# Output, up and down projections of a gated block: from plain tiled products to seven half-size block products in one sequence over all tokens

## The reference

```
h = RMSNorm(x)
q_a | k_a | v_a | u_pool | q_mem = h @ w_in
y_attn = window attention; y_pool = pooling; y_mem = attention into mem
merged = sum_i sigmoid(h @ Wg_i + b_i) * (y_i @ w_branch_i)
x = x + merged @ w_out                                  # 1024 x 1024
x = x + relu(RMSNorm(x) @ w_up)**2 @ w_down             # 1024 x 4096, 4096 x 1024
out = RMSNorm(x)
```

## Time and profile before

| | |
|---|---|
| median of 3 runs | 2945.35 us (2944.4 to 2946.05) |
| the profiled execution, its time | 2946.49 us |
| its span, first to last instruction | 2944.8 us |
| PE busy | 2890.6 us (98%) |
| DVE, ACT, POOL busy | 1350.5, 961.5, 195.3 us |
| DMA | 293.99 MB, mean 100 GB/s |
| mean granted TensorE clock | 0.995 |

### The profile page before, as it was taken

The page is one execution under the profiler, slowest core; times in us unless marked ns, Lnnn a source line. Parts: engine busy times, 40 slices in busy tenths (PEclk is TensorE's granted clock), DMA queues, the critical chain, the costliest instruction groups (busy, mean ns, idle before and its releaser), DMA issues.

```text
span 2944.8 us, 35670 instructions
## 1 busy us (share of the span) xinstructions
PE 2890.6 (98%) x13481; PEld 2391.0 (81%) x13481; DVE 1350.5 (46%) x1625; ACT 961.5 (33%) x1425; POOL 195.3 (7%) x191
## 2 busy tenths in 40 slices
PE   8999999999999999999999999999999999999998
PEld 7788888888778888888877888888887888888886
DVE  4643344445364245444446334544444632454444
ACT  5542332222353233212245323322224432422223
POOL 0101110000010111000001011000000001100000
PEclk9999999999999999999999999999999999999999
DMA  5123333332322342333232234223323222432332
GB/s 187 61 83 97 121 122 100 100 98 88 101 62 86 100 157 86 100 100 100 86 102 69 79 100 157 91 95 100 100 86 102 69 86 93 157 99 88 99 100 86
DMA packets 290347, 293.99 MB, mean 100 GB/s; under 512 B 9704, under 2 KB 285212, under 8 KB 290204
## 3 DMA queue, kind: packets, MB, share of 16 engines
q1 hardware_dynamic: 287900, 283.71, 30.3%
q0 software_dynamic: 2304, 8.39, 0.7%
HBM read 283.67 MB, written 8.39 MB: 99 GB/s over the span
## 4 chain that ended last, share of the span: by engine, by line
PE 90%; issue 5%; DVE 2%; POOL 1%; ACT 1%; DMA 0%; DVEq 0%; POOLq 0%; ACTq 0%
PE ps L993 29%; PE ps L995 28%; PE ps L994 28%; PE ps L998 1%; POOL sq_sum L971 1%; PE ps L1145 1%; PE ps L1128 1%; PE ps L1116 1%; PE ps L1089 0%; ACT sq L357 0%; DVE u_lo L806 0%; DVE scores L733 0%; DVE out_tm L897 0%; DVE scores L715 0%; DVE h_lo L656 0%
## 5 line engine op out<-in xcount | busy, mean ns | idle before, releaser
L993 PE MATMUL ps<-h_hi,w_hi 128*128 128x512 f32 x2240 | 885.2, 395 | 12.7 <-issue 12.7
L995 PE MATMUL ps<-h_hi,w_lo 128*128 128x512 f32 x2240 | 874.7, 390 | 0.0
L994 PE MATMUL ps<-h_lo,w_hi 128*128 128x512 f32 x2240 | 874.4, 390 | 0.0
L615 DVE TENSOR_TENSOR w_lo<-stage,w_hi 128x2048 fp32r<-128x2048 f32 (+1 forms) x269 | 559.6, 2080 | 641.6 <-ACT w_hi L357 641.6
L357 ACT ACTIVATE w_hi<-stage 128x2048 fp32r<-128x2048 f32 (+2 forms) x287 | 485.1, 1693 | 526.0 <-PE ps L995 524.6
L993 PE MATMUL ps<-u_hi,w_hi 128*128 128x512 f32 x1280 | 501.0, 391 | 5.5 <-DVE u_lo L806 5.5
L993 PEld LDWEIGHTS ps<-h_hi,w_hi 128*128 128x128 f32 x2240 | 422.3, 189 | 101.9 <-issue 14.3
L995 PE MATMUL ps<-u_hi,w_lo 128*128 128x512 f32 x1280 | 498.4, 389 | 0.0
L994 PE MATMUL ps<-u_lo,w_hi 128*128 128x512 f32 x1280 | 498.1, 389 | 0.0
L995 PEld LDWEIGHTS ps<-h_hi,w_lo 128*128 128x128 f32 x2240 | 422.1, 188 | 88.8
L994 PEld LDWEIGHTS ps<-h_lo,w_hi 128*128 128x128 f32 x2240 | 422.6, 189 | 86.7 <-issue 1.0
(11 more groups left out here) (153 smaller groups left out, 1837.9 us busy)
## 6 DMA issues: line engine op xcount, KB each, us to landing
stage<-in_w_up SPq DMA_DIRECT2D x128, 512.0 KB, 4.7
stage<-in_w_down SPq DMA_DIRECT2D x128, 512.0 KB, 4.0
stage<-in_w_gate SPq DMA_DIRECT2D x96, 512.0 KB, 4.5
stage<-in_w_in SPq DMA_DIRECT2D x60, 512.0 KB, 4.8
stage<-in_w_out SPq DMA_DIRECT2D x32, 512.0 KB, 4.1
x_tm<-in_x SPq DMA_DIRECT2D x5, 2048.0 KB, 9.6
stage<-in_w_branch_attn SPq DMA_DIRECT2D x32, 256.0 KB, 4.0
stage<-in_w_branch_pool SPq DMA_DIRECT2D x32, 256.0 KB, 3.0
```

The source lines that it names most:

```text
L615: v.tensor_tensor(w_lo[:, slot, 0:kt, :], stage[:, slot, 0:kt, :], w_hi[:, slot, 0:kt, :].bitcast(F32), ALU.subtract).then_inc(lo_done, 1)
L993: mm(dst, wh, xh, start=first, stop=False)
L994: mm(dst, wh, xl, start=False, stop=False)
L995: return mm(dst, wl, xh, start=False, stop=last)
```

## The change

The four blocks now stop after the merge (32 pieces in a block). POOL stores each block's merged tiles to DRAM (`mrg_d`). `x_next` brings the next block's rows during the merge, and their eight transposes follow the last merge piece. The factor 0.5 of the merge moves into the halves of the branches.

After the four blocks a second part does the three projections for all tokens, in straight-line code: seven jobs (`FIRST`), 72 pieces. Job 0 is `w_out` (8 pieces), jobs 1 and 2 are `w_up` for one half of the tokens each (16 pieces each), jobs 3 to 6 are quarters of `w_down`'s rows (8 pieces each). A job keeps a 1024 x 1024 operand resident; a piece is the other operand's 1024 x 256 columns, and gives 256 x 1024 of output. Both are cut into 2 x 2 blocks, and the output is made from seven block products instead of eight (the scheme of sums of Strassen in Winograd's form). A block product is four k-tiles of `product`, 12 matmuls with 512 columns. The seven are named after the piece's block or sum of blocks: A11, S2, S1, S3, A12, A22, S4, in this order on PE.

- POOL makes the piece's sums S1 to S4 (`s_sums`) and, for jobs 0 and 3 to 6, adds the four output tiles to the rows (`add_tile`), which are loaded from and stored to DRAM (`load_rows`, `store_rows`). ACT and DVE make the halves of the seven piece blocks (`s_split`, `s_low`; six slots). DVE takes the products out of PSUM (`take_u2`, `take_c22`, `take_c11`, `take_c21`, `take_c12`), and in jobs 1 and 2 also squares the positive part of four tiles (`relu_sq`), which SP stores to `up_d`.
- For a job, the resident operand comes in four quarters: three into `src`, the fourth, B21, into `res_raw`. DVE makes T1 and T2 (`t1`, `t2`), POOL T3 and T4 (`t3`, `t4`, 128x2048 elements each), and ACT and DVE make the halves of the seven resident blocks (`r_split`, `r_low`, 128x2048 each). Quarter 0 is issued when two pieces of the job before are left, quarters 1 and 2 in the last piece, B21 after its product A12.
- Pieces of `piece_f` have one buffer: the next is issued when all sums of the one before are made and its first six blocks are split. SP's queue is in order: in jobs 3 to 5 the store of the finished rows stands ahead of it and waits for POOL's four additions (`row_add`).
- Job 0's rows are normalised (`scale_tile`), transposed by PE (`rows_across`, 16 transposes a piece) and stored to `ht_d`; the last job's rows are normalised and stored to the output.

The core of the diff:

```diff
-W_MERGE, W_OUT, W_MLP = 16, 32, 36
-PIECES = 68
+W_MERGE = 16
+PIECES = 32
 PIECES0 = 4
 
...
+N_OUT, N_UP, N_DOWN = 8, 16, 8
+FIRST = [0, 8, 24, 40, 48, 56, 64]
+NQT = 72
+SLOTS = 6
+PROD = 7
+A11, S2, S1, S3, A12, A22, S4 = range(PROD)
...
+    res_hi = sb("res_hi", [P, PROD, 4, TB], F32R)
+    lo_at = off[0]
+    res_lo = sb("res_lo", [P, PROD, 4, TB], F32R)
+    res_raw = at("res_raw", [P, PROD, 4, TB], F32, lo_at)
+    src = sb("src", [P, 3, 4, TB])
+    piece_f = sb("piece_f", [P, KT, PC])
+    s_hi = sb("s_hi", [P, SLOTS, 4, P], F32R)
+    s_lo = sb("s_lo", [P, SLOTS, 4, P], F32R)
+    s_sum = sb("s_sum", [P, 2, 4, P])
...
+    S_SRC = {A11: quarter(0, 0), S2: s_sum[:, 1], S1: s_sum[:, 0], S3: quarter(0, 1), A12: quarter(1, 0), A22: quarter(1, 1),
+             S4: s_sum[:, 1]}
+    R_SRC = {0: src[:, 0], 1: src[:, 0], 2: res_raw[:, 2], 3: src[:, 1], 4: res_raw[:, 4], 5: res_raw[:, 5], 6: src[:, 2]}
+    S_NEED = {S1: 1, S2: 2, S3: 3, S4: 4}
+    R_HI_ORDER = (0, 2, 1, 3, 4, 6, 5)
+    R_LO_ORDER = (0, 1, 2, 3, 6, 4, 5)
+    U2, U3, U4, C22, C11, C21, C12 = range(1, 8)
+    FREED = {S2: U2, S1: C22, S3: U3, A12: C11, A22: C21, S4: C12}
+    def acc(n, i):
+        return ps[:, (PROD * n + i) % 6, :]
...
-                    load(j % 2, w_outv[:, :, j * PC:(j + 1) * PC], lo0 + (W_OUT + j))
-                    sp.wait_ge(tile_done, t0 + (G_MERGE if j < 2 else G_OUT + 4 * (j - 2) + 2))
-                    sp.wait_ge(x_ld, 16)
-                    sp.dma_start(xres[:, j % 2], x_rows[:, bass.ds(row_q, TT), j * PC:(j + 1) * PC])\
-                        .then_inc(xres_ld[j % 2], 16)
-                sp.wait_ge(tile_done, t0 + G_OUT)
-                sp.wait_ge(x_ld, 16)
-                sp.dma_start(x_tm[:], x_rows[:, bass.ds(row_n, TT), :]).then_inc(x_ld, 16)
...
+                        sp.wait_ge(tile_done, t0 + G_MERGE)
+                        sp.dma_start(x_next[:], x_rows[:, bass.ds(row_n, TT), :]).then_inc(x_ld, 16)
...
+            sp.wait_ge(phase, 3)
+            for j in range(4):
+                sp.wait_ge(mrg_st[j], 16 * NBLK)
+            sp.wait_ge(x_ld, 16 * (NBLK + 1))
...
+            load_quarter(0, 0)
+            load_piece(0)
+            load_quarter(0, 1)
+            load_quarter(0, 2)
+            load_b21(0)
+            load_rows(0)
+            for n in range(NQT + 1):
+                if squares(n - 1):
+                    store_up(n - 1, 3, c12, 0, 1)
+                if adds_rows(n - 1) and not is_final(n - 1):
+                    sp.wait_ge(row_add, 4 * row_quartets(n))
+                    store_rows(n - 1, rows_v)
+                if n + 1 < NQT:
+                    sp.wait_ge(s_lo_done, PROD * n + 6)
+                    sp.wait_ge(s_done, 4 * n + 4)
+                    load_piece(n + 1)
+                if is_final(n - 1):
+                    sp.wait_ge(fin_rdy, n - FIRST[6])
+                    store_rows(n - 1, out_v)
...
+                if adds_rows(n + 1) and not 0 < n < N_OUT:
+                    m = n + 1
+                    if m >= FIRST[3]:
...
+                    sp.wait_ge(row_st[row_slot(m)], 16 * slot_uses(m))
+                    load_rows(m)
+                if n < NQT and starts(n + 2):
+                    j = job_of(n) + 1
+                    sp.wait_ge(r_lo_done, PROD * j)
+                    sp.wait_ge(t_pool, 2 * j)
+                    if j < 3:
+                        for s in range(2):
+                            sp.wait_ge(ht_st[s], 16 * 4 * j)
+                    load_quarter(j, 0)
+                if n + 1 < NQT and starts(n + 1):
+                    load_quarter(job_of(n + 1), 1)
+                    load_quarter(job_of(n + 1), 2)
+                if squares(n):
+                    store_up(n, 0, c22, 1, 1)
+                    store_up(n, 1, c11, 0, 0)
+                if n + 1 < NQT and starts(n + 1):
+                    sp.wait_ge(prod, PROD * n + A12 + 1)
+                    load_b21(job_of(n + 1))
...
+            def s_split(n, i):
+                g = PROD * n + i
+                if n >= NQT:
+                    return
+                if i == 0:
+                    act.wait_ge(pc_ld, 16 * (n + 1))
+                if i in S_NEED:
+                    act.wait_ge(s_done, 4 * n + S_NEED[i])
+                if g >= SLOTS:
+                    act.wait_ge(prod, g - SLOTS + 1)
+                op(s_hi[:, ring_slot(n, i)], S_SRC[i], ACT.Copy).then_inc(s_hi_done, 1)
+            def r_split(j, s):
+                if s in (0, 6):
+                    act.wait_ge(src_ld[0 if s == 0 else 2], 16 * (j + 1))
+                elif s == 4:
+                    act.wait_ge(b21_ld, 16 * (j + 1))
+                elif s in (1, 2):
+                    act.wait_ge(t_done, 2 * j + (2 if s == 1 else 1))
+                else:
+                    act.wait_ge(t_pool, 2 * j + (1 if s == 3 else 2))
+                if j:
+                    act.wait_ge(prod, PROD * (FIRST[j] - 1) + s + 1)
+                op(res_hi[:, s], R_SRC[s], ACT.Copy).then_inc(r_hi_done, 1)
...
+            def s_low(n, i):
+                if n >= NQT:
+                    return
+                dve.wait_ge(s_hi_done, PROD * n + i + 1)
+                slot = ring_slot(n, i)
+                v.tensor_tensor(s_lo[:, slot], S_SRC[i], s_hi[:, slot].bitcast(F32), ALU.subtract).then_inc(s_lo_done, 1)
+            def r_low(j, s):
+                dve.wait_ge(r_hi_done, PROD * j + R_HI_ORDER.index(s) + 1)
+                if s == 4:
+                    dve.wait_ge(t_pool, 2 * j + 2)
+                elif s == 2:
+                    dve.wait_ge(t_done, 2 * j + 2)
+                v.tensor_tensor(res_lo[:, s], R_SRC[s], res_hi[:, s].bitcast(F32), ALU.subtract).then_inc(r_lo_done, 1)
+            def t1(j):
+                for i in range(2):
+                    dve.wait_ge(src_ld[i], 16 * (j + 1))
+                if j:
+                    dve.wait_ge(prod, PROD * (FIRST[j] - 1) + S1 + 1)
+                v.tensor_tensor(res_raw[:, 2], src[:, 1], src[:, 0], ALU.subtract).then_inc(t_done, 1)
+            def t2(j):
+                dve.wait_ge(src_ld[2], 16 * (j + 1))
+                dve.wait_ge(r_lo_done, PROD * j + 1)
+                dve.wait_ge(t_done, 2 * j + 1)
+                v.tensor_tensor(src[:, 0], src[:, 2], res_raw[:, 2], ALU.subtract).then_inc(t_done, 1)
...
+            def take_u2(n):
+                dve.wait_ge(prod, PROD * n + S2 + 1)
+                dve.wait_ge(ev_act, n + 1)
+                if adds_rows(n - 1):
+                    dve.wait_ge(row_add, 4 * row_quartets(n))
+                v.tensor_tensor(u2[:], p1[:], acc(n, S2), ALU.add).then_inc(ev_dve, 1)
+            def take_c22(n):
+                dve.wait_ge(prod, PROD * n + S3 + 1)
+                dve.wait_ge(ev_dve, 7 * n + U2)
+                v.tensor_tensor(u3[:], u2[:], acc(n, S3), ALU.add).then_inc(ev_dve, 1)
+                dve.wait_ge(ev_dve, 7 * n + U3)
+                v.tensor_tensor(u2[:], u2[:], acc(n, S1), ALU.add).then_inc(ev_dve, 1)
+                if squares(n - 1):
+                    dve.wait_ge(up_st[0], 16 * up_quartets(n))
+                v.tensor_tensor(c22[:], u3[:], acc(n, S1), ALU.add).then_inc(ev_dve, 1)
...
+            for n in range(NQT):
+                j, first, last = job_of(n), starts(n), starts(n + 1) and n + 1 < NQT
+                if first:
+                    r_low(j, 3)
+                s_low(n, 6)
+                take_u2(n)
+                if last:
+                    r_low(j + 1, 0)
+                    t1(j + 1)
...
+                if has_norm(n - 1):
+                    row_var(n - 1)
+                s_low(n + 1, 0)
+                if has_norm(n - 1):
+                    scale_tile(n - 1)
+                if first:
+                    r_low(j, 6)
+                    r_low(j, 4)
+                    r_low(j, 5)
+                take_c22(n)
+                if last:
+                    t2(j + 1)
+                relu_sq(n, C22)
+                s_low(n + 1, 1)
+                s_low(n + 1, 2)
+                take_c11(n)
+                relu_sq(n, C11)
+                if last:
+                    r_low(j + 1, 1)
+                take_ht(n - 1, 0)
+                s_low(n + 1, 3)
+                take_c21(n)
+                relu_sq(n, C21)
+                take_ht(n - 1, 1)
+                s_low(n + 1, 4)
+                if last:
+                    r_low(j + 1, 2)
+                take_c12(n)
+                relu_sq(n, C12)
+                s_low(n + 1, 5)
...
+                    pool.wait_ge(sum_rdy, sj + 5)
+                    pool.dma_start(mrg_v[:, 2 * j:2 * j + 2, bass.ds(b * TB, TB)], resid[:, 2 * j:2 * j + 2, :])\
+                        .then_inc(mrg_st[j], 16)
...
+                add_tile(n - 1, C12, 0, 1)
+                if first:
+                    t4(j)
+                row_rms(n - 1)
+                s_sums(n + 1, S1)
+                s_sums(n + 1, S2)
+                s_sums(n + 1, S3)
```

(41 more changed lines are left out.)

709 lines of the change are left out of this document (397 added, 312 removed).

## The result

The changed kernel takes 3029.19 us (median; 3023.81 to 3030.45) where the kernel before took 2945.7 on the same chip: ratio 1.028, 95% interval 1.0262 to 1.0298. The forecast was 2969 us, +0.8%. The time lies within the stated range (2865 to 3035), but the change costs 83 us where the sum had about 23. The sign and most of the walk hold; the stalls are 60 us more than the sum had.

What follows compares the result with a forecast made beforehand. Bound taken: TensorE's count of matmuls. First part 1314.4, start 59, 71 pieces 1351.1, stalls 24 + 26 + 10 + 156, clock 13, end 14 sum to 2967.5, plus 1.7 outside the span: 2969 us; range 2865 to 3035.

Steps and rivals of the forecast that it cites:

- the term of job 0: Job 0's pieces: 16 transposes cost 2.1 us a piece and waits about 1, so 8 x 3 = 24 us.
- the lower clock: TensorE's clock halves after idling: 2.2 us lost at each boundary that no later wait absorbs, 13 us in all.
- the rows' store before `scale_tile`: A wait not walked; the prediction called itself wrong if it held DVE in every piece; no size given.
- Steady down pieces: Jobs 3 to 5: the loop through the single piece buffer takes 21.3 us, 2.3 over PE; 26 us in all.
- the jobs' slack takes up: Jobs 3 to 5: 15 us of the 18 x 2.3 us loop excess is absorbed by slack, leaving 26.
- The start: Second part's start: the first piece ends 59 us after the last merge.
- Boundaries: Six changes of job: stalls of 28 us at three and 24 us at three, 156 us in all.
- The late quarters: Job boundaries: DVE stands before T1 until quarter 1 lands; early quarters would give some 10 us less each.
- late quarters cost nothing: Rival, boundaries: DVE would stand anyway until S3's product, so -27 us, 2942 us; chance 0.10.
- The engines overlap better: Rival: POOL and DVE exclude each other rarely, so down pieces stay under 19.03 and boundaries shorten; 2874 us; chance 0.30.
- the loop binds everywhere: Rival: the piece buffer's loop binds in down, up and job 0 pieces, without slack; 3041 us; chance 0.20.
- Matmuls removed: Three projections: 6048 large matmuls instead of 6912; the 864 fewer at 0.2266 us are worth 196 us at most.

Runs made afterwards that it cites:

- e3: Changed kernel with the finished rows scaled ahead of the next piece's first low half: 3003.63 us, ratio 1.0204.
- e6: e1, e2 and e3 together, with job 0's transposes and their evictions one product later: 2917.65 us, ratio 0.9908.
- e4: Changed kernel with GpSimd's sums cut to 8 of 128 columns and row additions to 32 of 512, T3 and T4 whole: 2907.95 us, ratio 0.9871.
- e9: e8 with the later transposes of e6 added: 2874.74 us, ratio 0.9762.
- e10: e9 with the next piece's load ahead of the rows' store in job 0 too: 2874.62 us, ratio 0.9763.
- e2: Changed kernel with the next piece's load issued ahead of the finished rows' store in jobs 3 to 5: 2987.02 us, ratio 1.0143.
- e8: e1, e2, e3 and e7 together, with resident low halves 6 and 4 ahead of the next piece's first low half: 2890.77 us, ratio 0.9813.
- e1: Changed kernel with all three quarters of the next resident operand issued together, two pieces before the job's end: 3001.2 us, ratio 1.0189.
- e11: e9 with the four additions to the rows done by VectorE instead of GpSimd: 2862.96 us, ratio 0.9724.
- e7: Changed kernel with T3 and T4 moved from GpSimd to VectorE: 3007.91 us, ratio 1.0209.

## Why the prediction came out as it did

- **The step that failed** is the term of job 0, 16 transposes a piece, "so 2.1, and about 1 of waits: 8 x 3 = 24", with its boundary of 24: 48 predicted, 85.5 measured, 37 of the 60 us missed. The transposes were priced by their length, and their waits were put at about 1 without a walk. But they stand inside TensorE's order, between A12 and A22, and the first eight wait there for a scaling that stands behind a low half that waits for the landing, the second eight for the eviction of the first: the trace shows 44 us of waiting before them. That puts TensorE into the buffer's loop: landing, low half, scaling, transposes, A22, eviction to `ht`, transposes, S4, last addition, store, load. e3 (-2.7 us a piece) and e6 (-2.4) each take out a link, and e4 (-3.9) shows that GpSimd's operations are in this loop too. Of the 27.0 us of a piece, TensorE stands 4.5. As an estimate from the two stretches under e6, 1.5 more are the lower clock, which the prediction charged at boundaries alone, and 2.0 the transposes. With e3 and e6 both in, a piece of job 0 costs 3.1 us over 19.03. That this is the predicted 3 confirms the sizes for an order that the kernel does not have; it does not confirm the term.
- **What the prediction named.** It said that it would be wrong if "the rows' store before `scale_tile`" held VectorE in every piece. The scaling was indeed the place, but not that store the reason: it had landed 4.8 us before the scaling began. The low half ahead of the scaling, waiting for the next piece, was not named. Waits of the scaling for that store are 3.3 us in all in e3, 2.0 in e9 and 20.1 in e10.
- **Steady down pieces.** The loop was sized right. In the piece shown under e2 it is 12.9 us from the landing to the store's issue (walked 13.7), 0.6 to the load's (none walked) and 7.5 to the landing (7.6), and e2 shows that it is this loop. What failed are the 15 us "that the jobs' slack takes up". The slack is there, for TensorE runs ahead by up to 10 us, but it is borrowed: the boundary takes it back by a longer stand of TensorE, and the sum subtracted it from the pieces without adding it there. In the table it shows as 15.6 of the 60 us.
- **The start** was 10 us short. The long sums on POOL stretched the halves there too: T4 was given at 1345.85, and the resident low half for S2 behind it took 6.24 us where a row of 2.3 was used. e8 took 7 of the 10 away. Timeline of the kernel after:

```profile
1345.85 4.96 POOL L1358 TENSOR_TENSOR res_raw<-res_raw,src 128x2048 f32<-128x2048 f32 x1
...
1346.73 6.24 DVE L1109 TENSOR_TENSOR res_lo<-src,res_hi 128x2048 fp32r<-128x2048 f32 x1 [0.29 <-ACT res_hi L591]
```

- **Boundaries.** Between evictions, and with 2.2 us of clock each, four of the six are within 1 us of the walk (26.2, 26.3, 30.5 and 29.4 us over two pieces, for 26.2 and 30.2), the last is 3.7 over, job 0's belongs to the step above. The order of the waits and A12 (58.0 against 57.7) were right. T3 was set at 5.2 and took 4.6; it changed nothing, since T2 behind it and the landing of piece 49 kept their times.
- **The late quarters** cost 28 us (e1). The text said "some 10 less each" for early ones, 60 in all. The mechanism was right, the size twice too large, because T3 takes T1's place. The rival "late quarters cost nothing" falls.
- **"The engines overlap better"** falls: low halves average 0.98 and 1.13 us, and e4 gives 121 us back. The larger rival, "the loop binds everywhere", was nearest in time (3041, outside the stated range) and right that the loop binds in job 0 and leaves no slack. It priced job 0 at 9 us more, which is too little, and the up pieces at 20, where they run at 19.1; so its nearness is in part luck.
- **Matmuls removed.** The pace is as before: pieces 9 to 38 run at 19.1 us for 84 matmuls. The 196 us were there. Since the span grew by 83 all the same, what was added to it is 279 us (the prediction writes "about 210"; its own terms make 219); e11 gets 166 of them back.

## What to carry to other kernels

When a change turns a kernel bound by one engine into one that hands work around, write down the loop through each single buffer with every in-order engine in it, the waiting TensorE too, and look for instructions and transfers whose inputs are there but which stand in order behind one that waits: four such orders cost 28, 42, 26 and 15 us here, and they added. Slack ahead of such a loop is only lent: what one stage saves by it, the next stop takes back. Try GpSimd's sums of two SBUF operands on VectorE before judging that VectorE is full. Taking one wait away is not its length gained: e1 and e7 gave back half and less of what was expected, and e8, with what stood behind the wait moved too, 42 of 60.
